# A transformer block's attention with full 128x128 matmuls, probabilities stationary and sums divided four heads at a time

## What is computed

```python
# attention a (MoBA, one block), per head; b (MLA) has q, k of 96 columns and its own v
s = einsum('qd,kd->qk', q, k) * scale
s = where(kpos <= qpos, s, -inf)
p = softmax(s)
o = einsum('qk,kd->qd', p, v)
...
gates  = sigmoid(gate_logits + b_gate)
merged = gates[:, :1024] * (o_a @ w_branch_a) + gates[:, 1024:] * (o_b @ w_branch_b)
x = x + rms_norm(merged @ w_out, g_post_mix)
```

## Time and profile before

| | us |
|---|---|
| median of 3 runs | 1022.56 (1022.08 to 1023.8) |
| the profiled execution | 1022.38 |
| its span in the trace | 1020.6 |
| PE busy | 988.2 |
| DVE busy | 718.9 |
| ACT busy | 473.4 |

### The profile page before, as it was taken

One profiled execution on the slowest core, in us unless ns is written; L12 is line 12 of the kernel. 1 busy time (PEld: TensorE's weight loads), 2 busy tenths in 40 slices (PEclk: granted clock), 3 DMA queues, 4 the chain that ended last, 5 costly groups with the idle time before them and its releaser, 6 DMA issues.

```text
span 1020.6 us, 13346 instructions
## 1 busy us (share of the span) xinstructions
PE 988.2 (97%) x5444; PEld 851.7 (83%) x5444; DVE 718.9 (70%) x788; ACT 473.4 (46%) x545; POOL 75.9 (7%) x70
## 2 busy tenths in 40 slices
PE   7999999999999999999989999999989999999997
PEld 7886787878888887998878888888879878888886
DVE  5565775867776666668866767677679977666674
ACT  4575546544534344542123634344359845434341
POOL 0100000000000001006530000000003100000000
PEclk9999999999999999999999999999999999999999
DMA  7764333636464562753303665555435547555531
GB/s 258 254 224 165 124 125 103 233 105 237 172 244 165 188 223 107 266 170 119 124 1 125 227 212 184 199 189 171 146 139 186 180 153 281 191 206 168 203 124 41
DMA packets 27132, 176.87 MB, mean 173 GB/s; under 512 B 3392, under 2 KB 3648, under 8 KB 7488
## 3 DMA queue, kind: packets, MB, share of 16 engines
q1 hardware_dynamic: 26784, 174.98, 48.6%
q10 hardware_dynamic: 288, 1.05, 0.3%
HBM read 174.97 MB, written 1.05 MB: 172 GB/s over the span
## 4 chain that ended last, share of the span: by engine, by line
PE 41%; DVE 6%; issue 2%; ACT 1%; DMA 1%; POOL 0%; POOLq 0%; DVEq 0%; ACTq 0%; SPq 0%
PE ps L1553 14%; PE ps L1556 7%; PE ps L1526 6%; PE ps L1527 6%; PE ps L1528 6%; DVE wL L929 2%; PE ps L1884 1%; DVE FF L1457 1%; PE ps L1572 1%; DVE FF L1433 1%; DMA raw<-w_stream 1%; DVE RR L941 0%; ACT wH L515 0%; DVE FF L1453 0%; DVE FF L1446 0%
## 5 line engine op out<-in xcount | busy, mean ns | idle before, releaser
L929 DVE TENSOR_TENSOR wL<-raw,wH 128x2048 fp32r<-128x2048 f32 (+2 forms) x158 | 354.7, 2256 | 119.8 <-ACT wH L515 119.7
L515 ACT ACTIVATE wH<-raw 128x2048 fp32r<-128x2048 f32 (+2 forms) x158 | 292.7, 1861 | 118.2 <-PE ps L1556 55.3
L1553 PE MATMUL ps<-aHL,wH 128*128 128x512 f32 x864 | 215.8, 392 | 0.0
L1553 PEld LDWEIGHTS ps<-aHL,wH 128*128 128x128 f32 x864 | 157.2, 189 | 29.4
L1526 PE MATMUL ps<-wL,RR 128*128 128x512 f32 (+1 forms) x384 | 149.8, 390 | 0.3 <-DVE RR L941 0.3
L1527 PE MATMUL ps<-wH,RR 128*128 128x512 f32 (+1 forms) x384 | 149.1, 388 | 0.0
L1528 PE MATMUL ps<-wH,RR 128*128 128x512 f32 (+1 forms) x384 | 148.8, 388 | 0.0
L1526 PE MATMUL ps<-wL,aHL 128*128 128x512 f32 (+2 forms) x304 | 122.1, 402 | 6.1 <-DVE aHL L941 3.8
L1556 PEld LDWEIGHTS ps<-aHL,wL 128*128 128x128 f32 x864 | 117.9, 190 | 8.4
L1556 PE MATMUL ps<-aHL,wL 128*128 128x256 f32 x864 | 120.5, 282 | 0.0
L1528 PE MATMUL ps<-wH,aHL 128*128 128x512 f32 (+2 forms) x304 | 117.6, 387 | 0.0
(11 more groups left out here) (216 smaller groups left out, 1128.5 us busy)
## 6 DMA issues: line engine op xcount, KB each, us to landing
raw<-w_stream SPq DMA_DIRECT2D x152, 1024.0 KB, 4.9
raw<-w_stream SPq DMA_DIRECT2D x6, 512.0 KB, 3.6
FF<-rows_in SPq DMA_DIRECT2D x5, 512.0 KB, 7.6
raw<-w_stream SPq DMA_DIRECT2D x4, 576.0 KB, 5.0
bc<-rows_in SPq DMA_DIRECT2D x4, 512.0 KB, 7.5
raw<-w_stream SPq DMA_DIRECT2D x2, 768.0 KB, 9.1
xn<-rows_in SPq DMA_DIRECT2D x1, 1024.0 KB, 4.5
out<-xn SPq DMA_DIRECT2D x4, 256.0 KB, 2.0
```

The costliest lines, as they stand in the source:

```text
L515: e.activation(weight_slot(i)[0][:, 0:wd], raw[:, i % NRAW, 0:wd], ACT.Copy).then_inc(hi, 1)
L929: e.tensor_tensor(l[:, 0:wd], raw[:, i % NRAW, 0:wd], h[:, 0:wd].bitcast(F32), ALU.subtract).then_inc(lo, 1)
L1553: e.matmul(ps[:, b, :], h[:, cs[k]], aHL[:, k].rearrange("p i t -> p (i t)"), start=k == 0, stop=False)
```

## The change

Scores: the queries of a are kept in two tiles, `mqT[0]` with the even heads' rows and zeros below, `mqT[1]` with the odd heads' rows and zeros above; keys stay as they were, and the stationary operand is 128x128. `lqT` and `lkT` get 128 rows, the last 32 zero. POOL writes the zeros in four memsets behind its fourth latent power. ACT fills `mqT` with two copies of 64 partitions for each tile in place of one of 128.

Mix: the turned probabilities are stationary (128x128) and 64 value columns stream; four heads of both tiles fill one bank. The probabilities are not divided. `out_rows` on DVE takes eight reciprocals and multiplies the bank's 128x512 rows by them, `flip_out` on PE turns the result with four transposes, `out_in` (ACT) and `out_low` (DVE) write its halves, once in four heads. `scale_rows`, `mix_in` and `mix_low` are gone.

Order: 16 steps, each with its gate piece; `flip_probs(i - 1)` and `mix(i - 2)` stand one step earlier. The branches are a00, a01, a10, a11, b00, b01, b10, b11, with `flip_probs(15)`, `mix(14)`, `mix(15)` and `flip_out(3)` among the a pieces; the chunks follow this order, and banks are given by three tables. The two sigmoids now split by branch, and the merge is in two parts.

```diff
             def scores(i):
-                    r = slice(64 * (h % 2), 64 * (h % 2) + 64)
-                    q, k = mqT[r, h // 2, :], mkT[r, h // 2, :]
+                    q, k = mqT[h % 2][:, h // 2, :], mkT[:, h // 2, :]
...
             def mix(i):
-                e.matmul(ps[r, b, 0:128], v[:, 0, :], pT[j][:, 0:128], start=True, stop=True)
-                e.matmul(ps[r, b, 128:256], v[:, 0, :], pT[j][:, 128:256], start=True, stop=False)
-                e.matmul(ps[r, b, 128:256], v[:, 1, :], pT[j][:, 256:384], start=False, stop=True).then_inc(mixed, 1)
+                e.matmul(o[0], pT[j][:, 0:128], v[:, 0, :], start=True, stop=True)
+                e.matmul(o[1], pT[j][:, 128:256], v[:, 0, :], start=True, stop=False)
+                e.matmul(o[1], pT[j][:, 256:384], v[:, 1, :], start=False, stop=True).then_inc(mixed, 1)
+
+            def flip_out(g):
+                e.wait_ge(o_rows, g + 1)
+                for n in range(2):
+                    for t in range(2):
+                        last = e.transpose(ps[:, g % 2, 256 * n + 128 * t:256 * n + 128 * t + 128],
+                                           o_row[:, 256 * t + 128 * n:256 * t + 128 * n + 128], ident[:, :])
...
+            e.wait_ge(powered, POWER["lat", 3])
+            for n, tile in enumerate((mqT[0][64:128, :, :], mqT[1][0:64, :, :], lkT[96:128, :, :], lqT[96:128, :, :])):
+                e.memset(tile, 0.0).then_inc(padded, 1)
...
-                from_flip(("mq", t, 0), (mqT,), 4 + t, 4)
+                for odd in range(2):
+                    r = slice(64 * odd, 64 * odd + 64)
+                    turned = e.activation(mqT[odd][r, :, TOK[t]], ps[r, 4 + t, :].rearrange("p (k t) -> p k t", k=4),
+                                          ACT.Copy)
...
-            def scale_rows(i):
-                linked(e.reciprocal(m[:, 4:6], m[:, 2:4]))
-                e.tensor_scalar(sm[j][:, 0:128], sm[j][:, 0:128], m[:, 4:5], None, ALU.mult).then_inc(scaled, 1)
-                e.tensor_scalar(sm[j][:, 128:384], sm[j][:, 128:384], m[:, 5:6], None, ALU.mult).then_inc(scaled, 1)
...
+            def out_rows(g):
+                linked(e.reciprocal(inv, linked_sum))
+                e.wait_ge(mixed, 4 * g + 4)
+                e.tensor_tensor(o_row.rearrange("p (t h d) -> p t h d", t=2, h=4),
+                                ps[:, g % 2, :].rearrange("p (t h d) -> p t h d", t=2, h=4),
+                                inv.rearrange("p (t h) -> p t h", t=2).unsqueeze(3).to_broadcast([128, 2, 4, 64]),
+                                ALU.mult).then_inc(o_rows, 1)
```

More of the change, by code:

```diff
@@ L653, in _, with out_in @@
[L653 to L663 removed]
+            def out_in(g):
+                e.wait_ge(o_flip, g + 1)
+                e.activation(oT[g // 2][0][:, 2 * (g % 2):2 * (g % 2) + 2, :], halves(g % 2), ACT.Copy).then_inc(o_hi, 1)
@@ new lines, in gate_sigmoid @@
+            def gate_sigmoid(n):
+                e.wait_ge(gated, 4 * n + 4)
+                c = slice(1024 * n, 1024 * n + 1024)
+                e.activation(gates[:, :, c], gates[:, :, c], ACT.Sigmoid).then_inc(gate_done, 1)
+            for i in range(16):
+                exps(i)
+                if i < 2:
+                    split(17 + i)
+                elif i in (3, 4, 7, 8, 11, 12):
+                    split(17 + 2 * ((i + 1) // 4) + (i + 1) % 4)
+                if i >= 1:
+                    probs_in(i - 1)
+                if i in (6, 10, 14):
+                    out_in((i - 6) // 4)
@@ L665, in stage_norm @@
+            gate_sigmoid(0)
+            probs_in(15)
+            split(25)
+            out_in(3)
+            split(26)
+            gate_sigmoid(1)
+            split(28)
+            from_flip(("merged", 0, 0), act, MERGED_BANK[0][0], 4)
+            split(29)
+            from_flip(("merged", 0, 1), act, MERGED_BANK[0][1], 4)
+            split(31)
+            for g in range(2):
+                from_flip(("merged", 1, g), act, MERGED_BANK[1][g], 4)
             def stage_norm(name, post, t, y_done):
@@ new lines, in out_low @@
+            def out_low(g):
+                o_h, o_l = (o[:, 2 * (g % 2):2 * (g % 2) + 2, :] for o in oT[g // 2])
+                e.wait_ge(o_hi, g + 1)
+                low_half(o_l, halves(g % 2), o_h).then_inc(o_lo, 1)
+            for i in range(16):
+                score_rows(i)
+                if i in (6, 10, 14):
+                    out_rows((i - 6) // 4)
+                if i in (7, 11, 15):
+                    out_low((i - 7) // 4)
+                if 1 <= i < 3:
+                    split(16 + i)
+                elif i in (4, 5, 8, 9, 12, 13):
+                    split(17 + 2 * (i // 4) + i % 4)
+                if i % 4 >= 2:
+                    gate_rows(i // 4, i % 4 - 2)
@@ L1133, in merge, with gate_a @@
+            def gate_a(n, t):
                 if t == 0:
@@ L1725, in gate_piece @@
                     last.then_inc(half, 1)
-            for i in range(19):
-                if i < 16:
-                    scores(i)
-                if i < 14:
-                    gate_piece(i)
-                elif 15 <= i < 17:
-                    gate_piece(i - 1)
-                if 2 <= i < 18:
-                    flip_probs(i - 2)
-                if i >= 3:
-                    mix(i - 3)
-            def branch(name, n, t, bank):
+            for i in range(16):
+                scores(i)
+                gate_piece(i)
+                if i >= 1:
+                    flip_probs(i - 1)
+                if i >= 2:
+                    mix(i - 2)
+                if i in (6, 10, 14):
+                    flip_out((i - 6) // 4)
@@ L1750, in _ @@
+            e.wait_ge(o_lo, 3)
+            branch("a", 0, 0)
+            flip_probs(15)
+            mix(14)
+            e.wait_ge(score_in, 15)
+            branch("a", 0, 1)
+            mix(15)
+            e.wait_ge(score_in, 16)
+            branch("a", 1, 0)
+            flip_out(3)
+            e.wait_ge(p_in, 15)
+            branch("a", 1, 1)
+            e.wait_ge(o_hi, 4)
+            e.wait_ge(o_lo, 4)
             e.wait_ge(gated, 7)
-            branch("b", 0, 0, 2)
-            branch("a", 0, 1, 1)
+            branch("b", 0, 0)
```

210 lines of the change are left out of this document (96 added, 114 removed).

## The result

| | before | after |
|---|---|---|
| median of 4 runs | 1022.98 us (1022.08 to 1023.8) | 1013.12 us (1012.22 to 1014.64) |
| the profiled execution | 1022.38 | 1012.22 |
| its span | 1020.6 | 1010.4 |
| start of the first scores | 83.63 | 83.83 |
| first w_out matmul | 186.86 | 178.95 |

The ratio is 0.9905, with an interval of 0.9888 to 0.9922: faster, by 9.9 us. The forecast was 1015.4 us, at least 1013.8. So the sign and most of the gain came as worked out, and the gain was larger than the range allowed.

What follows compares the result with a forecast made beforehand. PE, busy 97% of the span, was taken as the bound. The terms -1.6 - 5.4 + 1.8 - 1.95 = -7.15 us put the profiled execution at 1015.2 and the forecast at 1015.4 us, range 1013.8 to 1020.5.

Steps and rivals of the forecast that it cites:

- A: Attention a's 64-row score tile: zero-padding it to a full tile saves 0.20 us, 8 times, -1.6 us.
- B: Mix's 64-column tile: full tiles with stationary probabilities save 0.34 us a head, 16 times, -5.4 us.
- Term C: flip_out's sixteen added transposes cost 0.45 us for each four, +1.8 us in all (1.6 to 2.2).
- Term D: Three PE waits, two for divided probabilities and one for the gate bias, go: 0.42 + 0.54 + 0.99, -1.95 us.
- the walk: out_rows on DVE ahead of flip_out is hidden behind PE's gate piece, by 0.7 us plus turn and mix.
- DVE did not bound the branch stage: Rival that DVE's low halves delay the branch stage, 1 to 2 us given back: 1016.5 to 1017.5 us; chance 0.10.
- my walk of the new order: Behind the branches, PE meets the third w_out chunk's low half from DVE within 0.2 us of its end.
- What cost nothing: POOL's memsets, ACT's split query copies and the dropped scale_rows cost nothing; lost cover at the copies up to 0.5 us.
- all is as before and moves as a block: After the first w_out matmul (186.86 us) nothing changes; almost all the gain lies between 83 and 187 us.

Runs made afterwards that it cites:

- e13: Changed kernel, but every product that began on half of its turned operand, w_out too, waits for both halves; 1019.03 us, ratio 0.9947.
- before + 5: Kernel before with five idle float32 matmuls ahead of the turn of probabilities in step 9; 1025.6 us, ratio 1.0016.
- before, three places filled: Kernel before with 30 idle matmuls in PE's waits near 504, 526 and 763 us; 1021.3 us, ratio 0.9978.
- after + 5: Changed kernel with five idle float32 matmuls ahead of the turn of probabilities in step 9; 1016.19 us, ratio 0.9929.
- before, one place filled: Kernel before with ten idle matmuls in PE's waits at the HGRN heads' normalization; 1022.61 us, ratio 0.9989.
- one and three places filled: Changed kernel with ten idle matmuls at the HGRN heads' normalization, 1013.64 us; with 30 idle matmuls at three places, 1013.32 us.
- after + 11: Changed kernel with eleven idle float32 matmuls ahead of the turn of probabilities in step 9; 1017.71 us, ratio 0.9945.
- before + 11: Kernel before with eleven idle float32 matmuls ahead of the turn of probabilities in step 9; 1026.77 us, ratio 1.003.
- e14: Kernel before, but hgrn_w_out alone starts once the first half of its turned operand is there; 1022.68 us, ratio 0.9989.

## Why the prediction was right and wrong

**Terms A and B: right together, A too small alone.** Eight steps of a fell by 0.56 us and eight of b by 0.31: 8 x 0.56 + 8 x 0.31 = 6.96 us, where the prediction had 7.0. B is 5.3 by its own experiment (5.4). A is 2.6 and not 1.6, as far as it can be told alone: the two share the switch from mix into scores, and whichever is undone first gets 0.11 us a head of a (0.33 + 0.34 - 0.56). The 6.96 takes every step for a steady one; the first steps of a fell by less. Also 0.87 us from scores to the second gate matmul was too low, 0.94 was measured, and mix was 0.62 instead of 0.65.

**Term C: right.** 1.7 us against 1.8. The bank's division on DVE was hidden, as the walk said. One `out_rows` of the changed kernel, timeline of DVE (L1104 opens `score_rows`, L1129 is the 128x512 pass):

```profile
127.64 0.56 DVE L1104 SCALAR_TENSOR_TENSOR FF<-ps,amask 128x384 f32<-128x384 f32 x1 [1.01 <-PE ps L1722]
...
129.05 0.69 DVE L1129 TENSOR_TENSOR FF<-ps,st 128x512 f32<-128x512 f32 x1
```

It ends at 129.74, and `flip_out` begins at 131.15: 1.4 us of cover.

**Term D: right in kind, too small.** All three waits went. With them went 0.3 us behind the divided probabilities that the wait rows don't hold (the stretch fell by 1.71, the two waits are 1.41), and a wait in the branch stage of the kernel before that I had not counted:

```profile
183.61 0.66 PE L1572 MATMUL ps<-ident,xn 128*128 128x128 f32 x4 [0.29 <-DVE xn L1149]
```

The term is 1.71 + 0.54 + 0.29 = 2.54 us in place of 1.95. With A, B and C it makes 6.96 + 2.54 - 1.7 = 7.8; the stretch shows 8.11, so 0.3 us stay without a place. DVE did not bound the branch stage, but by my walk of the new order it should nearly have; the half wait, which I hadn't read, gave it 1.7 us of cover.

**What cost nothing** almost did. The first scores start 0.20 us later, 0.09 of it a longer wait for the query copies, within the 0.5 us of the prediction.

**The step that failed** is the sentence behind the terms, that after the first w_out matmul "all is as before and moves as a block". Two things were wrong with it. The change itself goes on behind that matmul: the half wait brings 0.6 us at hgrn_w_out, and this could have been read from the code. And a block that is moved doesn't keep its clock: the kernel before pays 1.35 us for a fall at 529 us that the changed one doesn't pay. Of the 3.0 us by which the two profiles differ beyond the 7.15 of the sum, 0.76 lie ahead of w_out (term D above all), the rest behind it. The whole account by the two profiles is 8.11 - 0.20 (later start) = 7.91 at w_out, 7.76 at 531 us, + 0.6 + 1.35 = 9.7, and 0.4 in small steps.

That the fall is no accident of two profiles shows in the lowest runs. Starts and DVE waits as above move a run by some 1 us either way (the profile of e13 starts 1.2 us early), so a distance of 1 us by itself says little. Take 1012.2 us, the changed kernel's lowest, as its time without inner falls, and add the difference in work that the traces show (the kernel before: + 7.8 + 0.6 = 8.4):

| kernel | lowest run | sum of the work | over it |
|---|---|---|---|
| after, a on 64 rows | 1014.92 | 1012.2 + 2.6 = 1014.8 | 0.1 |
| after, values stationary | 1017.79 | + 5.3 = 1017.5 | 0.3 |
| after, one transpose | 1010.84 | - 1.27 = 1010.9 | -0.1 |
| before + 5 | 1021.54 | + 8.4 + 1.14 = 1021.7 | -0.2 |
| before, three places filled | 1020.83 | + 8.4 = 1020.6 | 0.2 |
| before | 1021.95 | + 8.4 = 1020.6 | 1.4 |
| before, half wait | 1021.52 | + 7.8 = 1020.0 | 1.5 |
| after, both halves at hgrn_w_out | 1014.49 | + 0.6 = 1012.8 | 1.7 |
| after + 5 | 1015.12 | + 1.18 = 1013.4 | 1.7 |
| after, wide values | 1014.71 | + 0.14 = 1012.3 | 2.4 |

The first five had a run at the sum of their work. By the same sum the variants left out of the table lie over it by 0.3 (before, one place filled), 0.5 (before without the division), 0.6 and 0.7 (after, one and three places filled), 1.2 (after + 11, and every half wait undone) and 2.2 (before + 11). The kernel before never had a run at its sum in 85; it stood at least 1.4 us above, the price of the one fall in its profile, and came down when the idle time was filled. The mean granted clock, recorded for each run, says the same: none of the 81 runs of the kernel before beside the experiments is over 0.995, while the changed kernel reaches 0.997, and so do the kernel before without the division, with five matmuls more and with three places filled.

So of the 9.9 us some 8.4 are the work of the change, which alone gives 1022.38 - 8.4 = 1014.0 us (1014.6 from the median), just inside the range. The rest is that fall and 0.4 us in small steps. That the changed kernel escapes the fall because it comes there earlier is argued, not shown. The range had no term for the clock, in either direction.

**What stays open:** what decides whether the clock falls behind a given wait. The two waits at hgrn_w_out, 1.09 and 1.57 us before and 1.08 and 1.57 in e13, had a fall behind them; with 1.08 and 0.97 us there was none in the changed kernel and one in e14. Four variants of the changed kernel that keep the short wait (64 rows, values stationary, wide values, one transpose) fell there too, so the short wait alone doesn't keep the clock up. The other falls came behind waits of 2.53 us (near 500 us, after + 5), 1.91 us (near 758 us, wide values) and 1.32 us (near 84 us, a on 64 rows). Open also is why the chunk near 190 us comes later in some executions, and the late start. No version was found that is clearly faster than the changed kernel.

## What to carry to other kernels

Where matmuls of unlike tile shapes alternate on PE, read the distance between starts at each switch: a 64-row or 64-column operand among full ones cost 0.33 us a head here, and padding with zeros to a full tile was nearly free (the first scores started 0.20 us later); a price read from two steps that share a switch is only a lower bound. Walk through every line of the diff for waits, also where a helper serves products far behind the change. And where short PE waits stand in the program, a shift of 1 us can give or take 1 to 3 us, through the clock and through waits for data that come and go: look at the granted clock in windows of 2 us, and give the range a term for it.

## What the runs showed of the hardware that was not expected

- A stationary operand's rows matter to its neighbours: 64 of 128 rows among full tiles cost 0.33 us a head, though the load is as long (184 to 188 ns against 192). With 96 rows the way out costs nothing: 0.25 us from L1684 to the gate matmul, as with 128.
- 128 and 64 moving columns cost nearly the same in float32 (0.67 and 0.62 us for the three products of mix).
- 1.2 us of idle matmuls raised the changed kernel's median by 3.1 us, 1.6 of it a fall and 0.8 a wait for DVE in the profiled execution; 30 idle matmuls put elsewhere lowered that of the kernel before by 1.9 us.
